# Convolution phases of a four-layer block: lower halves of 18 weight pieces per layer on GpSimd, and two of its twelve taps on VectorE

## The reference

```python
def conformer_conv_mixer(h, w_in, conv_w, conv_b, ln_g, ln_b, w_out):
    proj = h @ w_in
    val, glu_gate, z = jnp.split(proj, 3, axis=-1)
    u = val * jax.nn.sigmoid(glu_gate)
    u = causal_depthwise_conv(u, conv_w) + conv_b
    u = jax.nn.silu(layer_norm(u, ln_g, ln_b))
    return (u * jax.nn.silu(z)) @ w_out
```

## Time and profile before

| what | us |
|---|---|
| median of three runs | 1817.43 (1815.01 to 1819.13) |
| span of the profiled execution; the page gives no other time of its own | 1817.8 |
| TensorE busy (granted clock 0.989 in the mean) | 1747.3 |
| VectorE busy | 1446.8 |
| ScalarE busy | 1075.3 |
| GpSimd busy | 331.3 |
| first convolution phase, GpSimd's first to last add | 33.4 to 182.7 |
| second convolution phase | 781.1 to 932.0 |

### The profile page before, as it was taken

How to read it: one execution, slowest core, us unless ns; L and a number is a source line. 1 busy time by engine, 2 the same in 40 slices (tenths; PEclk the granted TensorE clock), 3 DMA queues, 4 the chain that set the end, 5 groups by cost and what they waited for, 6 DMA issues and landing times.

```text
span 1817.8 us, 30986 instructions
## 1 busy us (share of the span) xinstructions
PE 1747.3 (96%) x11636; PEld 1580.2 (87%) x11636; DVE 1446.8 (80%) x2710; ACT 1075.3 (59%) x2047; POOL 331.3 (18%) x412
## 2 busy tenths in 40 slices
PE   7998999999999999999989999999999999999997
PEld 6887778888889999988877989989999898989996
DVE  7999777877778878789977688787777778787667
ACT  6888575555454444468975556565555556565554
POOL 2999000000000000079950000020000300030000
PEclk9999999999999999999989999999999999999998
DMA  6444458864558888644335554445764443536552
GB/s 228 150 141 151 140 170 310 275 204 167 197 195 278 301 295 291 208 156 151 132 128 185 169 195 135 166 152 192 242 211 161 154 148 125 176 131 220 190 182 70
DMA packets 92741, 339.62 MB, mean 187 GB/s; under 512 B 10288, under 2 KB 10672, under 8 KB 91952
## 3 DMA queue, kind: packets, MB, share of 16 engines
q1 hardware_dynamic: 92592, 337.64, 55.2%
HBM read 336.55 MB, written 1.05 MB: 186 GB/s over the span
## 4 chain that ended last, share of the span: by engine, by line
PE 62%; DVE 15%; issue 10%; ACT 10%; POOL 2%; DMA 1%; SPq 0%; DVEq 0%; ACTq 0%; POOLq 0%
PE ps L103 60%; DVE wl L119 6%; ACT tmp L109 4%; ACT wh L112 2%; POOL B L119 2%; DVE B L119 2%; PE ps L106 2%; DVE tmp L129 1%; ACT B L109 1%; ACT os L112 1%; DVE raw L129 1%; DVE tmp L119 1%; ACT ps L109 1%; ACT XS L112 1%; DVE os L119 1%
## 5 line engine op out<-in xcount | busy, mean ns | idle before, releaser
L103 PE MATMUL ps<-XS,wh 128*128 128x256 f32 x4464 | 830.2, 288 | 10.6 <-DVE wl L119 9.4
L103 PEld LDWEIGHTS ps<-XS,wh 128*128 128x128 f32 x4464 | 707.4, 194 | 26.5 <-issue 14.3
L119 DVE TENSOR_TENSOR wl<-raw,wh 128x1024 fp32r<-128x1024 f32 x481 | 593.4, 1260 | 111.8 <-ACT wh L112 110.7
L103 PE MATMUL ps<-XS,wl 128*128 128x256 f32 x2232 | 636.1, 285 | 0.0
L112 ACT CAST wh<-raw 128x1024 fp32r<-128x1024 f32 x481 | 486.8, 1045 | 150.2 <-PE ps L103 140.7
L103 PEld LDWEIGHTS ps<-XS,wl 128*128 128x128 f32 x2232 | 432.1, 194 | 0.0
L119 POOL TENSOR_TENSOR B<-B,tmp 128x237 f32<-128x237 f32 (+11 forms) x384 | 287.1, 785 | 644.5 <-ACT tmp L109 644.4
L103 PE MATMUL ps<-wh,os 128*128 128x512 f32 x864 | 284.1, 394 | 12.6 <-DVE os L119 8.4
L129 DVE SCALAR_TENSOR_TENSOR ps<-B,C,ps 128x254 f32<-128x254 f32 (+16 forms) x544 | 211.7, 467 | 6.8 <-ACT ps L109 6.7
L103 PEld LDWEIGHTS ps<-wh,os 128*128 128x128 f32 x864 | 162.4, 188 | 51.9 <-DVE os L119 13.2
L103 PE MATMUL ps<-B,raw 128*128 128x256 f32 x832 | 183.9, 381 | 0.9 <-ACT B L109 0.9
(11 more groups left out here) (157 smaller groups left out, 1621.6 us busy)
## 6 DMA issues: line engine op xcount, KB each, us to landing
raw<-in_w SPq DMA_DIRECT2D x628, 512.0 KB, 4.4
B<-in_ln SPq DMA_DIRECT2D x4, 1024.0 KB, 6.0
C<-in_cst SPq DMA_DIRECT2D x1, 1103.5 KB, 10.2
X<-in_x SPq DMA_DIRECT2D x2, 512.0 KB, 5.6
out_x<-X SPq DMA_DIRECT2D x4, 256.0 KB, 2.5
cb<-in_cb SPq DMA_DIRECT2D x1, 512.0 KB, 12.8
pos<-in_pos SPq DMA_DIRECT2D x1, 160.0 KB, 2.3
raw<-in_w SPq DMA_DIRECT2D x1, 128.0 KB, 3.0
```

Of the source, the lines that this page charges most:

```text
L103: return NOTHING if self.e is None else self.e.matmul(*a, **k)
L119: return NOTHING if self.e is None else self.e.tensor_tensor(o, a, b, op)
```

## The change

`POOL_TAPS` goes from 12 to 10: in both layers GpSimd's adds and ScalarE's products for taps 10 and 11 go, and VectorE does these taps. The list of 29 taps is interleaved anew (19 to 10). 18 pieces a layer (v2 to v7 and z4 to z6, two units each) have their lower half made by GpSimd, at fixed items between its adds, with a semaphore of their own; TensorE and SyncE wait for it where they waited for VectorE's. VectorE's calls for these pieces go. The positions differ: the lower half of v{p+1}.1 stood behind item 8 and `conv_end` on VectorE, and stands behind item 4 on GpSimd; that of v{p+2}.0 stood behind item 20, and stands behind item 14.

```diff
-POOL_TAPS = 12
+POOL_TAPS = 10
...
+        self.on_pool = {self.at[f"a{j}.{x}.{n}"] for j in range(2) for x in [f"v{p}" for p in range(2, 8)] + ["z4", "z5", "z6"]
+                        for n in range(2)}
...
-                sp.wait_ge(*self.s["low"][j])
+                sp.wait_ge(*self.low(j))
...
-            if self.kind[i] == "split":
+            if self.kind[i] == "split" and i not in self.on_pool:
...
+    def low(self, i):
+
+        return self.s["poollow" if i in self.on_pool else "low"][i]
+
+    def pool_low(self, pool, name):
+        s, i = self.s, self.at[name]
+        hi = self.m["wh"][i % NHL][:, 0:self.wd[i]].bitcast(F32)
+        pool.wait_ge(*s["cast"][i])
+        pool.tt(self.m["wl"][i % NHL][:, 0:self.wd[i]], self.raw(i), hi, ALU.subtract).then_inc(s["poollow"].up(i), 1)
...
-        pe.wait_ge(*self.s["low"][i])
+        pe.wait_ge(*self.low(i))
...
-            if 1 <= p < 7:
-                self.feed_dve(dve, f"{A}.v{p + 1}.1", 0)
-            if p == 7:
-                self.feed_dve(dve, f"{A}.z5.0", 0)
             items(p, 8, 14)
             self.masks(dve, more)
-            if p == 7:
-                self.feed_dve(dve, f"{A}.z5.1", 0)
             items(p, 14, 20)
             self.masks(dve, more)
             if p < 7:
                 val(p + 1)
-            self.feed_dve(dve, f"{A}.v{p + 2}.0" if p < 6 else f"{A}.z{2 * p - 8}.0", 0)
             items(p, 20, 28)
             self.masks(dve, more)
-            if p >= 6:
-                self.feed_dve(dve, f"{A}.z{2 * p - 8}.1", 0)
             items(p, 28, 30)
...
         for p in range(8):
...
+            items(p, 0, 4)
+            if 1 <= p < 7:
+                self.pool_low(pool, f"{A}.v{p + 1}.1")
+            if p == 7:
+                self.pool_low(pool, f"{A}.z5.0")
+            items(p, 4, 10)
+            if p == 7:
+                self.pool_low(pool, f"{A}.z5.1")
+            items(p, 10, 14)
+            self.pool_low(pool, f"{A}.v{p + 2}.0" if p < 6 else f"{A}.z{2 * p - 8}.0")
+            items(p, 14, 22)
+            if p >= 6:
+                self.pool_low(pool, f"{A}.z{2 * p - 8}.1")
+            items(p, 22, 30)
```

More of the change, by code:

```diff
@@ L159 @@
     "low",
+    "poollow",
     "ada",
@@ L1076, in pool_a, with item, items @@
         U, V, Z = self.a_views()
+        order = self.taps()
         n = 0
-        for p in range(8):
[L1079 to L1092, removed]
+        before = {}
+        def item(p, x):
+            nonlocal n
+            if x == 0 or order[x - 1] >= POOL_TAPS:
+                return
+            k = order[x - 1]
+            sh, q = 30 - k, self.tmp[2 + n % 3]
+            for i in (2 * p, 2 * p + 1):
+                h = (i % 2) * T
+                pool.wait_ge(*s["tap"][A, i, k])
+                if i in before:
+                    pool.wait_ge(*s["poolconv"][A, "t", i, before[i]])
+                pool.tt(V[:, i, sh:T], V[:, i, sh:T], q[:, h + sh:h + T], ALU.add).then_inc(
+                    s["poolconv"].up((A, "t", i, k), (A, 2 * n + i % 2)), 1)
+                before[i] = k
+            n += 1
+        def items(p, a, b):
+            for x in range(a, b):
+                item(p, x)
+        for p in range(8):
+            items(p, 0, 4)
[12 more added lines that the diff above has]
+            items(p, 22, 30)
     def rope_views(self):
```

## The result

The changed kernel took 1847.76 us (median of four runs, 1847.49 to 1848.17) against 1817.76 before (median of four runs here): ratio 1.0167, 95% interval 1.0153 to 1.0182. I had forecast 1818.6 in a range up to 1828. It is slower by 30.0 us, and not by what I had made the slower rival of.

A forecast was written before the change was run, and what follows sets the result against it. GpSimd was taken to pace both convolution phases; -0.6 and +0.25 us by pairs plus +0.7 for the clock gave +0.35, by work and idle time +1.4; +1.2 taken on 1817.8 us less 0.4 for the median gave 1818.6 us, range 1814 to 1828.

The forecast's parts named there:

- the slower rival: GpSimd's lower half is dearer than 2.34 us, deciding from 2.41 us upward; at 2.5 us 1824.4 us; chance 0.31.
- Work on GpSimd: Per layer: 32 adds removed -20.8, hold-up by VectorE's lower halves -18.0, 18 lower halves added +42.1, sum +3.3 us.
- the relief of 1.0 us: In each layer's phase, 18 lower halves taken off VectorE each spare GpSimd 1.0 us of hold-up, 18.0 us.
- Idle time of GpSimd: In the two phases, idle time of 6.7 and 6.5 us goes; 3.1 and 4.2 us come in pair 0.
- The waits of 3.53, 1.65 and 1.42 us: GpSimd's waits, 3.53 us in the first layer's pair 4, 1.65 and 1.42 in the second layer, were counted as gained.
- its wait for the cast of v2.0: In pair 0 GpSimd idles before its first lower half, 3.1 us in the first layer, 4.2 in the second.
- The term for the clock: After the last statistics, z6.1's 24 matmuls at half clock take 5.1 us instead of 4.4: +0.7 us once.
- the 0.2% that I had called no change: Whole kernel: a measurement can tell about 0.2%, 3.6 us, from no change.
- + 1.4 for the masks of pair 2: In the first layer's phase, the masks of pair 2 add 1.4 us to GpSimd's time.
- the sum by pairs: GpSimd's pairs 1 to 5 take 17.4 us, pair 6 19.75, pair 7 22.1; layers change by -0.6 and +0.25 us.
- ScalarE's and VectorE's queues lose waits and gain none: In both phases, the change adds no wait to ScalarE's or VectorE's queue; no size given.
- One of my own signs of being wrong: In the phases, the prediction is wrong if TensorE waits for GpSimd's lower halves; its waits for lower halves forecast under 1 us.

The follow-up runs named there:

- three_near: The changed kernel with one GpSimd wait for its own last add at the end of each pair ahead of one with masks, three in all; 1819.54 us.
- no_masks: The changed kernel with the 12 masks within the phases filled with ones by a memset instead of the comparison of two SBUF operands; 1816.92 us.
- own_wait: The changed kernel with a GpSimd wait for its own last add before each lower half and at each pair's end, 80 in all; 1830.13 us.
- few_waits: The changed kernel with GpSimd waits for its own last add only in the pairs with masks, five in each of three pairs; 1822.75 us.
- two-engine kernels: Separate kernels of GpSimd adds and VectorE subtractions alone; at 232 columns a subtraction issued after 14 adds got in (1.15 us), after 15 it was shut out.

## Why the prediction was wrong

**Work on GpSimd: right.** The lower half at 2.34 (2.394 as a duration), the adds at 0.64, the relief of 1.0 us for each lower half taken from VectorE: pairs of 17.4, 19.8 and 22.1 us came out as summed. The rival that the lower half is dearer had most of my chance of slower, and it was not what happened.

**Idle time of GpSimd: right.** The waits of 3.53, 1.65 and 1.42 us are gone in three_near, and pair 0 keeps its wait for the cast of v2.0 (2.36 us in the changed kernel, at 42.56).

**With the masks out of the way the forecast holds.** 1818.6 was forecast; three_near, which is the change and three pauses, has 1819.54, and no_masks 1816.92. The term for the clock is there as well: in the changed kernel z6.1's matmuls of the first layer take 5.2 us (196.67 to 201.90, at a granted clock of 0.50 from 197.4 to 201.3), where I had 5.1. What is left of three_near over the kernel before, 1.0014 (1.0004 to 1.0024), lies within the 0.2% that I had called no change.

**The step that failed** is "+ 1.4 for the masks of pair 2" in the sum by pairs, and with it "ScalarE's and VectorE's queues lose waits and gain none". I priced a mask by what it costs GpSimd, 0.45 us by my own rows (the sum has 0.35, which is a slip of 1.2 us in all), and never asked what GpSimd costs the mask. It was 15.06, 15.05 and 12.72 us for the first mask of each of the three pairs, and 10.26 us of standstill for GpSimd each time. One of my own signs of being wrong says so: TensorE waits for GpSimd's lower halves, 27.2 us. The rows that I had were all taken with VectorE's lower halves in between, and these are exactly what the change removes. I even wrote down that they hold GpSimd up for 18 us a layer and took it as pure loss; it was also what let the masks in. The Trainium skill, SBUF — State Buffer, "SBUF: two separate sides", says that a VectorE instruction with two SBUF inputs and a GpSimd instruction that reads SBUF exclude each other, and that the one that starts first has the port for its whole instruction. By that the mask would have waited for the instruction in flight, at most 2.4 us; the masks at 99.38 and 841.69 agree with it (2.37 us), but the one at 72.76 does not: 19 GpSimd instructions in a row passed it over. Had I weighed the rule, it would not have given this result: in three_near, where the masks wait for no more than that, none takes over 1.49 us.

**The price of the stop.** VectorE got lighter by about 12 us where 13 was forecast: 141.98 us busy in the first phase, 14.4 of them the mask's standing, against 139.60 (in pair 7 it now waits 10.9 us for GpSimd at the end), but slack over the phase doesn't help a queue that stands still within one pair: `val(3)` stood 17 instructions behind the mask, and ScalarE's whole next pair behind `val(3)`.

## What to carry to other kernels

Where GpSimd ran without a pause, with instructions that read and write SBUF, a VectorE instruction with two SBUF operands always got in when at most 13 GpSimd instructions had been done since the last pause or the last such instruction that got in, and never when there were 16 or more; then it lasted until GpSimd stopped. One wait of GpSimd for its own last instruction, a few instructions ahead of the place, is enough. It cost 0.12 us (own_wait, by the pair) to 0.27 us (few_waits has twelve waits more than three_near and took 3.2 us more). Before an instruction is taken off an engine, look at what it was interrupting.

## What the runs showed that I had not expected

- The limit is a count, 13 or 14 GpSimd instructions in the two-engine kernels, whether they follow one another every 0.39 us (116 columns) or every 2.3 us (1024). What it is that counts stays open: a drift that grows with each instruction and a queue that fills up would both look like this, and no run here tells them apart.
- VectorE instructions with one SBUF operand and one in PSUM are untouched beside the same row of GpSimd instructions: 0.69 us at 72.16, just ahead of the mask.
- The masks just after the stop, at 99.38 in the first layer and at 841.69 in the second, waited out a running lower half of GpSimd and took 2.37 us: that was the price of the exclusion below the limit.
